# The mix stage of a hybrid decoder step: operands split part by part between the tiles of the product above

## The chip, the cores and the metric

The program runs on one core of a Trainium2 chip. The metric is the time of one execution on the device, in microseconds; for several runs the median is given. A profiled execution gives one trace: each instruction's start and length on TensorE (PE, with its weight loads as PEld), VectorE (DVE), ScalarE (ACT), GpSimd (POOL) and on SyncE (SP), which issues nearly all of the DMAs, and the clock that TensorE was granted.

## The reference

One decoder layer is computed for 512 prompt tokens and 8 sample tokens, together 520 columns. Two token mixers run on one normalised input, a gated DeltaNet (result `o_a`) and a sparse attention (result `o_b`). Their results are merged, and a feed-forward part follows:

```python
gate_a, gate_b = jnp.split(jax.nn.sigmoid(g_merge), 2, axis=-1)
mixed = (gate_a * (o_a @ P['w_oa']) + gate_b * (o_b @ P['w_ob'])) @ P['w_out']
x = x + gt1 * _rms(mixed, P['norm_g'][1])
h = _rms(x, P['norm_g'][2]) * (1.0 + sc2) + sh2
gate, up = jnp.split(h @ P['w_gu'], 2, axis=-1)
x = x + gt2 * _rms((jax.nn.silu(gate) * up) @ P['w_down'], P['norm_g'][3])
```

All is float32; `w_oa`, `w_ob` and `w_out` are 1024 x 1024. The change lies in the second of these lines.

## The kernel before

Activations stand with features on the 128 partitions and tokens along them, as 8 parts (KD = 8) of 128 features x 520 tokens. A float32 product is made of three faster ones: each operand is split into a high half (a copy in the short format, made by ACT) and a low half (what is left, a subtraction on DVE), and PE adds up high x high, high x low and low x high. One output tile (128 features x 520 tokens) is thus 8 parts x 3 products x 2 halves of 260 tokens = 48 matmuls.

The class `Chain` runs a list of such products, its jobs. The stage "mix" is one chain of three jobs: `oa` (w_oa), `ob` (w_ob) and `out` (w_out), each of 2 passes x 4 tiles = 8 tiles. The gates are applied by DVE (L2169 for `oa`; L2174 and L2176 for `ob`, the second adds up the merged tile in `mg_sg`), and `mg_sg` is the operand of `out`.

Each engine has its own queue, and semaphores order them:

- SP (`run_loads`, L221): first the four loads of the gates from memory (L2161, 1040 KB each), then the weights. A ring has two places, each with the 256 columns of two tiles (1024 KB); a place is loaded again once DVE has split its second tile (semaphore `low`). The first two loads are issued in the stage ahead (L1556).
- ACT (`run_high`, L281): the high half of a tile's weights (`ahead`, L287; of the first tile L301) and of the operand's parts (`split`, L293). `ahead` for tile n waits until product n-2 is done, since there are two weight places.
- DVE (`run_low`, L306): the low half of the weights (`low`, L310) and of the parts (L316), and the gating.
- PE (`run_products`, L236): ahead of a job it waits for all of the job's 8 low parts (semaphore `x_low`), ahead of a tile for its low weights (`low`) and for a free place in PSUM (`free`).

The order of the splits is that of `splits_before` (L257). On ACT and DVE alike the stage begins with the 8 parts of `oa`, then the first tile's weights, then the 8 parts of `ob`, and then the loop of `steps` (L265): for each tile m, the weights of tile m+1 and then the gating of tile m. Between the loops of `ob` and `out` stand the 8 parts of `out`: they need the merged tiles, and ACT waits for the last of them before it splits the first (`extra[1]` at 8). The first gating of `oa` waits for all four gate loads:

```python
if i == 0:
    for n in range(4):
        v.wait_ge(gates_in[n], 16 + START)
```

The chains of the feed-forward part (`gu`, `dw`) use the same class with one job each and an operand that is split elsewhere (`source` is None).

Of the kernel before, what the change touches and what calls it, by code (L numbers as in the profile page):

```python
# [6 lines left out]
F32 = mybir.dt.float32  # L7
I32 = mybir.dt.int32
F32R = mybir.dt.float32r
ALU = mybir.AluOpType  # L10
ACT = mybir.ActivationFunctionType
# [4 lines left out]
KD = D // P  # L16
# [54 lines left out]
START = 1  # L71
# [97 lines left out]
class Chain:  # L169
# [66 lines left out]
    def run_products(self, pe):  # L236
        for job in self.jobs:
            xh, xl = job.pair
            if job.x:
                pe.wait_ge(self.x_low, job.x + START)  # L240
            with pe.Fori(0, job.iters) as t:
                for i in range(4):
                    b, j = i // 2, i % 2
                    pe.wait_ge(self.low, job.unit + 4 * t + i + 1 + START)
                    if not (job.halves and b):
                        pe.wait_ge(self.free[j], (job.freed + (t if job.halves else 2 * t + b)) + START)
                    k0 = b * job.K if job.halves else 0
                    for k in range(job.K):
                        for w, x in ((self.wh, xh), (self.wh, xl), (self.wl, xh)):
                            for c in range(2):  # L250
                                last = pe.matmul(  # L251
                                    self.ps[:, j, c, 0:HALF], w[:, j, k, :], x[:, k0 + k, c * HALF:(c + 1) * HALF],
                                    start=(k0 + k == 0 and w is self.wh and x is xh),
                                    stop=(k == job.K - 1 and w is self.wl and not (job.halves and b == 0)))
                    last.then_inc(self.done, 1)

    def splits_before(self, job):  # L257


        i = self.jobs.index(job)  # L260
        own = job.source is not None and (i == 0 or job.source_steps)
        after = self.jobs[i + 1:i + 2]
        return [job] if own else [], [j for j in after if j.source is not None and not j.source_steps]

    def steps(self, eng, job, ahead, empty):  # L265

        last_job = job is self.jobs[-1]
        with eng.Fori(0, job.iters - 1 if last_job else job.iters) as t:
            for i in range(4):
                ahead(job, t, i + 1)  # L270
                if empty:
                    empty(eng, self, job, t, i)
        if last_job:
            t = job.iters - 1
            for i in range(4):
                if i < 3:
                    ahead(job, t, i + 1)
                if empty:
                    empty(eng, self, job, t, i)

    def run_high(self, act):  # L281
        def ahead(job, t, i):
            n, b, j = job.unit + 4 * t + i, i // 2 % 2, i % 2
            if j == 0:
                act.wait_ge(self.loaded[b], (job.unit // 4 + t + i // 4 + 1) * 16 * self.per + START)
            act.wait_ge(self.done, n - 1 + START)
            act.activation(self.wh[:, j, 0:job.K], self.ring[:, b, 0:job.K, j * P:(j + 1) * P], ACT.Copy).then_inc(self.high, 1)  # L287

        def split(job):
            if job.source_steps:  # L290
                act.wait_ge(self.extra[1], job.source_steps + START)
            for k in range(KD):
                act.activation(job.pair[0][:, k], job.source[:, k], ACT.Copy).then_inc(self.x_high, 1)  # L293

        for job in self.jobs:
            own, after = self.splits_before(job)
            for other in own:
                split(other)
            if job is self.jobs[0]:
                act.wait_ge(self.loaded[0], 16 * self.per + START)  # L300
                act.activation(self.wh[:, 0, 0:job.K], self.ring[:, 0, 0:job.K, 0:P], ACT.Copy).then_inc(self.high, 1)  # L301
            for other in after:
                split(other)
            self.steps(act, job, ahead, job.act)

    def run_low(self, v):  # L306
        def low(job, t, i):
            n, b, j = job.unit + 4 * t + i, i // 2 % 2, i % 2
            v.wait_ge(self.high, n + 1 + START)
            v.tensor_tensor(self.wl[:, j, 0:job.K], self.ring[:, b, 0:job.K, j * P:(j + 1) * P],  # L310
                            self.wh[:, j, 0:job.K].bitcast(F32), ALU.subtract).then_inc(self.low, 1)

        def split(job):
            for k in range(KD):
                v.wait_ge(self.x_high, job.x - KD + k + 1 + START)
                v.tensor_tensor(job.pair[1][:, k], job.source[:, k], job.pair[0][:, k].bitcast(F32), ALU.subtract)\  # L316
                    .then_inc(self.x_low, 1)

        for job in self.jobs:
            own, after = self.splits_before(job)  # L320
            for other in own:
                split(other)
            if job is self.jobs[0]:
                low(job, 0, 0)
            for other in after:
                split(other)
            self.steps(v, job, low, job.dve)


def square_sums(ph, st):  # L330
# [1105 lines left out]
def attention(nc, io, st):  # L1436
# [4 lines left out]
    ident = consts[:, K_ID:K_ID + P]  # L1441
    steps = [(g, kv, i) for g in range(G) for kv in range(KV) for i in range(NCH)]
    N = len(steps)
    HALF_N = N // 2
    with Phase(nc, "att") as ph:
# [1149 lines left out]
```

## Time and profile before

| what | value |
|---|---|
| time, median of 3 runs | 1923.19 us (1921.03 to 2191.4) |
| profiled execution, its own time | 1924.08 us |
| its span, first to last instruction | 1922.6 us |
| TensorE's granted clock, mean over the span | 0.915 of full speed |
| PE busy | 1680.5 us (87%) |
| DVE busy | 744.9 us (39%) |
| ACT busy | 549.8 us (29%) |

A busy share is a mean over stages with different limits; for one stage, the waits and the order in time within it decide. Times in the rows are counted from the span's start. The mix stage runs from about 1295 us to 1455 us.

### The profile page before, as it was taken

The numbers are of one execution on the slowest core, as the hardware profiler recorded it, in microseconds if no ns is written. First come the engines' busy times: TensorE is split into PE (matmuls) and PEld (weight loads), VectorE is DVE, ScalarE is ACT, GpSimd is POOL, SyncE is SP. The second block draws the span as 40 slices with busy tenths as digits, with TensorE's granted clock in tenths as the row PEclk, the third lists the DMA queues.
The fourth block names the chain that finished last, engine by engine and source line by source line (L and its number), as shares of the span: only waits on it lengthen the run. The fifth ranks groups of instructions, "written<-read, shape, count | busy, mean of one in ns | idle before, by whom it ended". The sixth has DMA issues, their size and how long they took to land. (4 is left out here: it accounts for less than half of the span.)

```text
span 1922.6 us, 30114 instructions
## 1 busy us (share of the span) xinstructions
PE 1680.5 (87%) x11733; PEld 1484.7 (77%) x11733; DVE 744.9 (39%) x1290; ACT 549.8 (29%) x890; POOL 162.6 (8%) x177
## 2 busy tenths in 40 slices
PE   4899889889889889977788899898985899997996
PEld 2598888888888879866574454458985899997996
DVE  1244554554553421323414434434435333332223
ACT  3243333333333320210003333323133434332222
POOL 0012322322312201100000000000000000000000
PEclk9799989989999986986879999999997899998997
DMA  6422212212112132437532343244212233332211
GB/s 188 114 71 73 70 33 79 63 33 85 57 33 98 45 86 80 140 121 226 155 110 88 110 153 121 94 136 167 98 44 89 66 89 99 96 87 90 90 60 45
DMA packets 228688, 181.72 MB, mean 95 GB/s; under 512 B 8566, under 2 KB 221039, under 8 KB 228425
## 3 DMA queue, kind: packets, MB, share of 16 engines
q1 hardware_dynamic: 203434, 161.82, 27.8%
q10 hardware_dynamic: 25184, 18.96, 3.2%
q8 instruction: 43, 0.70, 0.1%
q14 instruction: 27, 0.22, 0.0%
HBM read 166.31 MB, written 23.02 MB: 98 GB/s over the span
## 5 line engine op out<-in xcount | busy, mean ns | idle before, releaser
L704 PE MATMUL dn_pg<-proj_xh,dn_wh 128*128 128x260 f32 x832 | 184.0, 297 | 6.5 <-DVE dn_wl L1003 6.0
L704 PE MATMUL dn_pg<-proj_xh,dn_wl 128*128 128x260 f32 x832 | 182.5, 296 | 0.0
L704 PE MATMUL dn_pg<-proj_xl,dn_wh 128*128 128x260 f32 x832 | 179.1, 293 | 0.0
L251 PE MATMUL gu_ps<-fh_xh,gu_wh 128*128 128x260 f32 x704 | 142.4, 284 | 19.1 <-DVE gu_wl L310 19.1
L251 PE MATMUL gu_ps<-fh_xh,gu_wl 128*128 128x260 f32 x704 | 142.4, 284 | 0.0
L251 PE MATMUL gu_ps<-fh_xl,gu_wh 128*128 128x260 f32 x704 | 142.3, 284 | 0.0
L704 PEld LDWEIGHTS dn_pg<-proj_xh,dn_wh 128*128 128x128 f32 x832 | 134.3, 195 | 8.3 <-DVE dn_wl L1003 7.1
L704 PEld LDWEIGHTS dn_pg<-proj_xh,dn_wl 128*128 128x128 f32 x832 | 134.2, 195 | 0.0
L704 PEld LDWEIGHTS dn_pg<-proj_xl,dn_wh 128*128 128x128 f32 x832 | 134.2, 195 | 0.0
L251 PEld LDWEIGHTS gu_ps<-fh_xh,gu_wh 128*128 128x128 f32 x704 | 109.2, 190 | 19.5 <-issue 19.5
L251 PEld LDWEIGHTS gu_ps<-fh_xh,gu_wl 128*128 128x128 f32 x704 | 109.2, 190 | 0.0
L251 PEld LDWEIGHTS gu_ps<-fh_xl,gu_wh 128*128 128x128 f32 x704 | 108.9, 189 | 0.0
L251 PE MATMUL mix_ps<-mg_xh,mix_wh 128*128 128x260 f32 x384 | 79.2, 288 | 16.5 <-DVE mix_wl L310 8.8
L310 DVE TENSOR_TENSOR gu_wl<-all_ring,gu_wh 128x1024 fp32r<-128x1024 f32 x44 | 53.9, 1226 | 83.1 <-ACT gu_wh L287 80.4
L251 PE MATMUL dw_ps<-ff_gated_high,dw_wh 128*128 128x260 f32 x352 | 72.2, 287 | 12.6 <-DVE dw_wl L310 12.6
L1718 ACT ACTIVATE att_lg<-att_lg,att_nm 128x128 f32<-128x128 f32 (+3 forms) x64 | 35.4, 553 | 163.9 <-DVE att_nm L1793 163.9
L251 PE MATMUL mix_ps<-mg_xl,mix_wh 128*128 128x260 f32 x384 | 78.7, 287 | 0.0
L251 PE MATMUL mix_ps<-mg_xh,mix_wl 128*128 128x260 f32 x384 | 78.6, 287 | 0.0
L251 PEld LDWEIGHTS mix_ps<-mg_xh,mix_wh 128*128 128x128 f32 x384 | 60.8, 193 | 17.0 <-issue 17.0
L1808 DVE COPY att_PT<-att_pT 128x256 f32<-128x256 f32 (+3 forms) x32 | 26.4, 824 | 117.7 <-PE att_pT L1581 117.7
L251 PE MATMUL dw_ps<-ff_gated_high,dw_wl 128*128 128x260 f32 x352 | 71.7, 285 | 0.0
L251 PE MATMUL dw_ps<-ff_gated_low,dw_wh 128*128 128x260 f32 x352 | 71.6, 285 | 0.0
(472 smaller groups left out, 3381.3 us busy)
## 6 DMA issues: line engine op xcount, KB each, us to landing
all_ring<-in_w_gu SPq DMA_DIRECT2D x44, 512.0 KB, 5.0
all_ring<-in_w_in SPq DMA_DIRECT2D x32, 512.0 KB, 6.9
att_ada<-in_w_ada SPq DMA_DIRECT2D x16, 1024.0 KB, 5.3
fd_ring<-in_w_down SPq DMA_DIRECT2D x8, 1408.0 KB, 6.2
all_ring<-in_w_in SPq DMA_DIRECT2D x10, 1024.0 KB, 5.3
fr_ada<-in_w_ada SPq DMA_DIRECT2D x8, 1024.0 KB, 8.7
dn_xs<-in_w_in SPq DMA_DIRECT2D x16, 512.0 KB, 3.7
all_ring<-in_cmp_w ACTq DMA_DIRECT2D x16, 512.0 KB, 4.5
```

The source lines that it names most:

```text
L251: last = pe.matmul(self.ps[:, j, c, 0:HALF], w[:, j, k, :], x[:, k0 + k, c * HALF:(c + 1) * HALF], start=(k0 + k == 0 and w is self.wh and ...
L310: v.tensor_tensor(self.wl[:, j, 0:job.K], self.ring[:, b, 0:job.K, j * P:(j + 1) * P], self.wh[:, j, 0:job.K].bitcast(F32), ALU.subtract). ...
L704: last = pe.matmul(pg[:, j, c, 0:HALF], w[:, j, k, :], x[:, k, c * HALF:(c + 1) * HALF], start=(k == 0 and term == 0), stop=(k == KD - 1 a ...
L1718: last = a.activation(row, row, ACT.Exp, bias=nm[:, n % 2, br:br + 1], accum_out=sm[:, n % 2, br:br + 1])
L1808: v.tensor_copy(PT[:, :, 0:i + 1, i * P:(i + 1) * P], pT[:, :, 0:i + 1, :]).then_inc(pt_ready, 1)
```

## The change

Four things are changed in `Chain`, and only chains whose jobs split their operand are touched, which is the mix stage alone.

- The first tile's weights are split ahead of the parts of `oa`, on ACT and on DVE.
- The 8 parts of `ob` are split one at a time in the 8 tiles of `oa`: part m after the weights of tile m+1 and the gating of tile m. The loop of `steps` is written out for `oa` and `ob`.
- The parts of `out` are split the same way in the tiles of `ob`, one tile late: part m-1 in tile m, and the last after the loop. ACT waits for the one merged tile that a part needs (`extra[1]` at k+1).
- PE no longer waits for all 8 low parts ahead of a job; in the first tile of each pass it waits ahead of each part for that part.

```diff
--- before.py
+++ after.py
@@ -236,8 +236,6 @@
     def run_products(self, pe):
         for job in self.jobs:
             xh, xl = job.pair
-            if job.x:
-                pe.wait_ge(self.x_low, job.x + START)
             with pe.Fori(0, job.iters) as t:
                 for i in range(4):
                     b, j = i // 2, i % 2
@@ -246,6 +244,8 @@
                         pe.wait_ge(self.free[j], (job.freed + (t if job.halves else 2 * t + b)) + START)
                     k0 = b * job.K if job.halves else 0
                     for k in range(job.K):
+                        if job.source is not None and i == 0:
+                            pe.wait_ge(self.x_low, job.x - KD + k + 1 + START)
                         for w, x in ((self.wh, xh), (self.wh, xl), (self.wl, xh)):
                             for c in range(2):
                                 last = pe.matmul(
@@ -259,12 +259,21 @@
 
         i = self.jobs.index(job)
         own = job.source is not None and (i == 0 or job.source_steps)
-        after = self.jobs[i + 1:i + 2]
-        return [job] if own else [], [j for j in after if j.source is not None and not j.source_steps]
-
-    def steps(self, eng, job, ahead, empty):
+        return [job] if own else []
+
+    def steps(self, eng, job, ahead, empty, part):
 
         last_job = job is self.jobs[-1]
+        follower = self.jobs[self.jobs.index(job) + 1:][:1]
+        if follower and follower[0].source is not None:
+            late = 1 if follower[0].source_steps else 0
+            for m in range(4 * job.iters):
+                ahead(job, m // 4, m % 4 + 1)
+                if empty:
+                    empty(eng, self, job, m // 4, m % 4)
+                if m >= late:
+                    part(follower[0], m - late)
+            return
         with eng.Fori(0, job.iters - 1 if last_job else job.iters) as t:
             for i in range(4):
                 ahead(job, t, i + 1)
@@ -286,22 +295,23 @@
             act.wait_ge(self.done, n - 1 + START)
             act.activation(self.wh[:, j, 0:job.K], self.ring[:, b, 0:job.K, j * P:(j + 1) * P], ACT.Copy).then_inc(self.high, 1)
 
+        def part(job, k):
+            if job.source_steps:
+                act.wait_ge(self.extra[1], k + 1 + START)
+            act.activation(job.pair[0][:, k], job.source[:, k], ACT.Copy).then_inc(self.x_high, 1)
+
         def split(job):
-            if job.source_steps:
-                act.wait_ge(self.extra[1], job.source_steps + START)
-            for k in range(KD):
-                act.activation(job.pair[0][:, k], job.source[:, k], ACT.Copy).then_inc(self.x_high, 1)
+            for k in range(KD - 1 if job.source_steps else 0, KD):
+                part(job, k)
 
         for job in self.jobs:
-            own, after = self.splits_before(job)
-            for other in own:
-                split(other)
+            own = self.splits_before(job)
             if job is self.jobs[0]:
                 act.wait_ge(self.loaded[0], 16 * self.per + START)
                 act.activation(self.wh[:, 0, 0:job.K], self.ring[:, 0, 0:job.K, 0:P], ACT.Copy).then_inc(self.high, 1)
-            for other in after:
+            for other in own:
                 split(other)
-            self.steps(act, job, ahead, job.act)
+            self.steps(act, job, ahead, job.act, part)
 
     def run_low(self, v):
         def low(job, t, i):
@@ -310,21 +320,22 @@
             v.tensor_tensor(self.wl[:, j, 0:job.K], self.ring[:, b, 0:job.K, j * P:(j + 1) * P],
                             self.wh[:, j, 0:job.K].bitcast(F32), ALU.subtract).then_inc(self.low, 1)
 
+        def part(job, k):
+            v.wait_ge(self.x_high, job.x - KD + k + 1 + START)
+            v.tensor_tensor(job.pair[1][:, k], job.source[:, k], job.pair[0][:, k].bitcast(F32), ALU.subtract)\
+                .then_inc(self.x_low, 1)
+
         def split(job):
-            for k in range(KD):
-                v.wait_ge(self.x_high, job.x - KD + k + 1 + START)
-                v.tensor_tensor(job.pair[1][:, k], job.source[:, k], job.pair[0][:, k].bitcast(F32), ALU.subtract)\
-                    .then_inc(self.x_low, 1)
+            for k in range(KD - 1 if job.source_steps else 0, KD):
+                part(job, k)
 
         for job in self.jobs:
-            own, after = self.splits_before(job)
+            own = self.splits_before(job)
+            if job is self.jobs[0]:
+                low(job, 0, 0)
             for other in own:
                 split(other)
-            if job is self.jobs[0]:
-                low(job, 0, 0)
-            for other in after:
-                split(other)
-            self.steps(v, job, low, job.dve)
+            self.steps(v, job, low, job.dve, part)
 
 
 def square_sums(ph, st):
```

## Rows read from the trace of the kernel before

**Rows 1.** The page's costliest groups: busy us, mean ns, idle before and who ended it.

```profile
L251 PE MATMUL mix_ps<-mg_xh,mix_wh 128*128 128x260 f32 x384 | 79.2, 288 | 16.5 <-DVE mix_wl L310 8.8
```

**Rows 2.** Timeline at the stage's start: start us, length us, engine, line, count, [idle before <-releaser].

```profile
1295.72 4.32 ACT L293 ACTIVATE mg_xh<-mixers_oaT 128x520 fp32r<-128x520 f32 x8 [0.77 <-PEq L108]
1296.39 4.97 DVE L316 TENSOR_TENSOR mg_xl<-mixers_oaT,mg_xh 128x520 fp32r<-128x520 f32 x8
1299.95 1.04 ACT L301 ACTIVATE mix_wh<-all_ring 128x1024 fp32r<-128x1024 f32 x1
1300.18 2.19 SPq L2161 DMA_DIRECT2D mg_sg<-merge_gates  x4
...
1301.28 1.21 DVE L310 TENSOR_TENSOR mix_wl<-all_ring,mix_wh 128x1024 fp32r<-128x1024 f32 x1
...
1302.62 0.80 PE L251 MATMUL mix_ps<-mg_xh,mix_wh 128*128 128x260 f32 x2 [8.11 <-DVE mix_wl L310]
```

**Rows 3.** Timelines of SP, DVE and PE: first weight loads, first gating, third tile.

```profile
1276.71 11.02 SPq L1556 DMA_DIRECT2D all_ring<-in_w_oa  x2
...
1315.11 0.70 DVE L2169 TENSOR_TENSOR mg_sg<-mix_ps,mg_sg 128x520 f32 x1 [6.60 <-DMA mg_sg<-merge_gates]
1315.73 1.22 DVE L310 TENSOR_TENSOR mix_wl<-all_ring,mix_wh 128x1024 fp32r<-128x1024 f32 x1
...
1317.07 0.50 PE L251 MATMUL mix_ps<-mg_xh,mix_wh 128*128 128x260 f32 x2 [0.67 <-DVE mix_wl L310]
```

**Rows 4.** DMA views: L2161's landings; issues at 1276 to 1288; issues at 1308.4 to 1308.8.

```profile
DMA to landing us min/median/max: 5.1/9.8/13.1
...
all_ring<-in_w_oa SPq DMA_DIRECT2D x2, 1024.0 KB, 5.3
...
all_ring<-in_w_oa SPq DMA_DIRECT2D x1, 1024.0 KB, 9.1
```

**Rows 5.** Timeline between the last tile of `ob` and the first of `out`.

```profile
1398.22 0.70 DVE L2174 TENSOR_TENSOR all_hT<-mix_ps,mg_sg 128x520 f32<-128x520 f32 x1 [3.08 <-PE mix_ps L251]
1399.08 0.70 DVE L2176 TENSOR_TENSOR mg_sg<-mg_sg,all_hT 128x520 f32 x1 [0.15 <-DVE all_hT L2174]
1399.82 4.32 ACT L293 ACTIVATE mg_xh<-mg_sg 128x520 fp32r<-128x520 f32 x8 [6.41 <-DVE mg_sg L2176]
...
1405.78 0.80 PE L251 MATMUL mix_ps<-mg_xh,mix_wh 128*128 128x260 f32 x2 [7.71 <-DVE mg_xl L316]
1406.38 0.64 PE L251 MATMUL mix_ps<-mg_xl,mix_wh 128*128 128x260 f32 x2
1406.81 0.64 PE L251 MATMUL mix_ps<-mg_xh,mix_wl 128*128 128x260 f32 x2
```

**Rows 6.** Windows on PE: length us, busy us (matmuls), granted clock, DMA share, GB/s.

```profile
1296.50:1297.00 0.50, 0.00 (x0) 0.81 0.00 0
...
1307.00:1307.50 0.50, 0.50 (x6) 0.95 1.07 399
...
1402.50:1402.75 0.25, 0.00 (x0) 0.75 0.00 0
...
1409.25:1409.50 0.25, 0.25 (x3) 0.60 0.99 348
...
1095.00:1095.50 0.50, 0.00 (x0) 0.93 1.08 385
```

**Rows 7.** Timeline, PE, in the attention stage: a shorter idle stretch.

```profile
1098.33 0.90 PE L1581 MATMUL att_pT<-all_consts,att_lg 128*128 128x128 f32 x3 [4.51 <-ACT att_lg L1726]
```

**Rows 8.** Timelines of one steady tile of `oa`, across its boundary: ACT, PE, PEld.

```profile
1351.97 1.07 ACT L287 ACTIVATE mix_wh<-all_ring 128x1024 fp32r<-128x1024 f32 x1 [4.70 <-PE mix_ps L251]
...
1346.01 0.40 PE L251 MATMUL mix_ps<-mg_xh,mix_wh 128*128 128x260 f32 x2
1346.25 0.41 PE L251 MATMUL mix_ps<-mg_xl,mix_wh 128*128 128x260 f32 x2
...
1345.89 0.31 PEld L251 LDWEIGHTS mix_ps<-mg_xh,mix_wh 128*128 128x128 f32 x2
```

## The prediction

> **What bounds the kernel now.** I read the page's costliest groups first: the first group of the mix stage's matmuls had 16.5 us of idle PE ahead of it [rows 1]. The timelines split that into three stops: 8.11 us at the stage's start [rows 2], 0.67 us ahead of the third tile [rows 3], 7.71 us between `ob` and `out` [rows 5]. Everywhere else in the stage PE is the bound: a steady tile takes 5.77 us (ACT's 1.07 us of work and 4.70 us of waiting for PE), its 48 matmuls start 0.12 us apart (two in 0.24), across the boundary of a tile too [rows 8]. So the change can act on these stops and on the clock around them, and on nothing else; the other chains run the same instructions as before.
>
> The reader should look at who ends the third stop of DVE, not of PE: at 1315.11 DVE had waited 6.60 us for the gate loads [rows 3]. In the kernel before PE is nearly as late as the gates (0.67 us of idle), so they hardly show in PE's rows. They decide what an earlier start is worth.
>
> **The boundary to `out`.** Before: the last product of `ob` ends at 1398.07 (1405.78 less 7.71), gating and addition take until 1399.78, then come 8 parts on ACT and DVE, and PE starts at 1405.78 [rows 5]. After: parts 0 to 5 are split during the tiles of `ob`, and PE goes on at once. It wants part 6 after 36 matmuls (1398.07 + 36 x 0.12 = 1402.4) and part 7 after 42 (1403.1). DVE does the gating at 1398.22, the addition at 1399.08, then part 6 until about 1400.4 (a part takes 4.97 / 8 = 0.62 us of its queue [rows 2]); ACT has split part 7 by 1399.82 + 0.6 = 1400.4, DVE's half of it ends at 1401.3. Both are early, by 2.0 and 1.8 us. Next late would be the second tile's weights: ACT to 1401.5, then 0.29 us to DVE (1299.95 + 1.04 to 1301.28 [rows 2]) and 1.22 us, 1403.0, against PE's need at 1398.07 + 5.77 = 1403.8. If that cover of 0.8 us were gone, PE would wait for the rest of it alone. So the whole 7.71 us go.
>
> The clock adds to it. It fell at 1402.62 (0.75 in a window of a quarter of a us means half of it at half speed) and came back at 1409.45 [rows 6], 3.67 us after PE began again. At half clock two matmuls take 0.43 us (1406.38 to 1406.81 [rows 5]), at full clock 0.24 [rows 8]: 3.67 x (1 - 0.24 / 0.43) = 1.62 us. Sum at this boundary: 7.71 + 1.62 = 9.33 us saved.
>
> **The start.** ACT begins at 1295.72 [rows 2] now with the first weights, which it doesn't have to wait for: their load was issued at 1276.71 [rows 3], a load of this kind lands 5.3 us later [rows 4]. High half to 1296.76, low half from 1297.05 to 1298.26, DVE's first part to 1298.95, and with 0.13 us from DVE to PE (1301.28 + 1.21 to 1302.62 [rows 2]) PE starts at 1299.1, 3.5 us earlier than now. It follows the parts without a stop: at half clock (the clock fell at 1296.81 [rows 6]) a part is 6 x 0.215 = 1.3 us on PE, and ACT and DVE make one in 0.62. Two tiles, with about 4 us of them at half clock as now, end at about 1299.1 + 7.55 + 5.77 = 1312.4.
>
> The third tile can't start then. Its low weights stand on DVE behind the gating of tile 0, and that waits for the gates. The change doesn't touch SP's issue at 1300.18 [rows 2]. The first ring load behind the gates does come 4.0 us earlier (it waits for the second tile's low weights, now at about 1298.26 + 8 x 0.62 + 1.21 = 1304.4, before at 1308.5). In the rows, loads land in order of issue: the gates at about 1314.8 (the last of the four, issued some 0.6 us ahead of 1302.4, took 13.1 us), the ring load at 1308.5 + 9.1 = 1317.6 [rows 2, 4], so I take 0 for this; the bound is 2.8 us, if the two shared the time. DVE gates at 1315.11 as before, and now has part 0 of `ob` ahead of the weights: 1315.73 becomes 1316.35, and PE starts its third tile at 1317.69 instead of 1317.07 [rows 3]. That is 0.62 us lost where a naive sum has a gain.
>
> PE has then stood still for 5.3 us. The clock fell 2.3 us after the last matmul in the first stop (1294.51 to 1296.81 [rows 2, 6]), 4.55 us after it in the one at `out` [rows 5, 6] and 1.6 us after it in a stop of 4.51 us in the attention stage (1093.82 to 1095.43 [rows 6, 7]); all three are shorter than 5.3, so I let it fall. After the stage's two restarts it was low for 4.43 us (1302.62 to 1307.05) and 3.67 us [rows 2, 5, 6]; the mean, 4.05, costs 4.05 x 0.442 = 1.79 us. Its bounds are 0 (no fall) and 1.96. Before, this place ran at full clock. Sum at the start: 0.62 + 1.79 = 2.41 us lost.
>
> **What is added and hidden.** In the tiles of `oa` ACT does 1.07 + 0.62 us and DVE 1.22 + 0.70 + 0.62 of the tile's 5.77; in those of `ob` DVE does 1.22 + 0.86 + 0.70 + 0.62 = 3.4 us. Behind ACT's new wait for a merged tile stand the weights of the tile after next, which wait for a product 5.77 us later than the one that gates this tile; behind DVE's wait for a part stand those weights' low halves, with 2.3 us to spare. Writing the loop out adds no instruction that runs. PE's new waits are 8 in each of 6 tiles; the first of each 8 falls together with the two waits that every tile has, so 42 stand between matmuls. The price of a wait that is already met has no row of its own; the nearest is the boundary of a tile, where two such waits leave the 0.12 us between matmuls as it is [rows 8]. So I take 0. The upper bound is a weight load that no longer overlaps: two of them take 0.31 us at 0.12 apart, so one takes 0.19 [rows 8], 42 x 0.19 = 8.0 us. A gain from these waits is excluded, since PE's work is the same.
>
> The Trainium skill (TensorE: Matmul & The Clock Gate, Step-by-step: what each phase is for) says that PE pulls the next weight load ahead of matmuls in flight; it doesn't say whether a wait between them stops that. If it did, the sum would be the second rival's; by the boundary rows it would stay as it is.
>
> **Sum.** 9.33 - 2.41 = 6.92 us saved: 1924.08 - 6.92 = 1917.2 for the profiled execution. The median of the runs is 0.89 below that execution, so 1916.3.
>
> **The rivals.**
> - The gates don't bind, because they land earlier or because DVE gets to the weights: PE goes on at 1312.4 instead of 1317.07, the clock stays up, 9.33 + 4.67 = 14.0 us, 1909.2. For it: the page names DVE's weights as what PE waited for, 8.8 us [rows 1]. Against it: DVE's 6.60 us for the gates [rows 3], and that DVE's order has the gating first.
> - The waits break PE's flow: 42 x 0.19 = 8.0 us lost, 8.0 - 6.92 = 1.1 us slower, 1924.3. The place is the first tile of each pass; it ends slower from 6.92 / 42 = 0.165 us for a wait on. For it: PE loads weights ahead [rows 8]; against it: the tile boundaries.
> - The clock doesn't fall in the new stop: 9.33 - 0.62 = 8.71 us, 1914.5. For it: in the stop at `out` it held for 4.55 us [rows 5, 6], near to 5.3.
> - The earlier ring load delays the gates by the full 2.8 us: 4.1 us saved, 1919.1. Against it: the order of landing [rows 4].
> - The change doesn't do what it says at `out`, because a part or the second tile's weights come late: each us over the covers named above is a us less.
>
> **How the numbers follow.** The forecast 0.60, the clock held 0.14, the gates delayed 0.08, the gates not binding 0.06, the waits 0.06, late parts and the rest 0.06. The range reaches from below the held clock to past the delayed gates, with about 1.5 us for the spread of runs (1921.03 and 1923.19 lie 2.2 apart): 1912.3 to 1921.3. No case comes near 2% (38 us, about what a measurement of this kernel can tell from no change): faster 0.01, same 0.98, slower 0.01.
>
> **What would show it.** In the changed trace: PE's first matmul of the stage about 3.5 us earlier; an idle stop of about 5 us ahead of the third tile, with DVE's gating of tile 0 still begun about 0.3 us after the last gate, and half clock behind it; matmuls 0.12 us apart through the first tiles of `ob` and `out`, and no stop between `ob` and `out`. The prediction is wrong if the third tile starts straight after the second, if the spacing widens every 6 matmuls in the first tile of a pass, or if PE stops at part 6 or 7 of `out`.

## The result, and the profile after

The changed kernel takes 1909.0 us (median of 4 runs, 1907.29 to 1914.12), the kernel before, with one run more, 1923.74 us. One of the four runs of the kernel before, 2191.4 us, was a slow one; it counts in that median (1923.19 without it) and not in the ratio. The ratio is 0.9934, with a 95% interval of 0.9907 to 0.9961: 0.7% less time. The forecast was 1916.3 with a range from 1912.3 to 1921.3, so the time lies below the range. The profiled execution went from 1924.08 to 1914.12 us, by 10.0, and its span from 1922.6 to 1912.8.

The page has, in place of the 16.5 us of [rows 1]:

```profile
L251 PE MATMUL mix_ps<-mg_xh,mix_wh 128*128 128x260 f32 x384 | 79.1, 288 | 7.6 <-DVE mg_xl L325 4.3
```

Timelines of the changed kernel at the stage's start (against [rows 2, 3]), columns as there:

```profile
1296.37 1.06 ACT L311 ACTIVATE mix_wh<-all_ring 128x1024 fp32r<-128x1024 f32 x1 [0.77 <-PEq L108]
1297.34 4.31 ACT L301 ACTIVATE mg_xh<-mixers_oaT 128x520 fp32r<-128x520 f32 x8
...
1298.61 4.96 DVE L325 TENSOR_TENSOR mg_xl<-mixers_oaT,mg_xh 128x520 fp32r<-128x520 f32 x8
1303.49 1.21 DVE L320 TENSOR_TENSOR mix_wl<-all_ring,mix_wh 128x1024 fp32r<-128x1024 f32 x1
1314.33 0.70 DVE L2180 TENSOR_TENSOR mg_sg<-mix_ps,mg_sg 128x520 f32<-128x520 f32 x1 [9.63 <-DMA mg_sg<-merge_gates]
1314.95 0.69 DVE L325 TENSOR_TENSOR mg_xl<-all_obT,mg_xh 128x520 fp32r<-128x520 f32 x1
1315.56 1.22 DVE L320 TENSOR_TENSOR mix_wl<-all_ring,mix_wh 128x1024 fp32r<-128x1024 f32 x1
...
1299.44 0.77 PE L251 MATMUL mix_ps<-mg_xh,mix_wh 128*128 128x260 f32 x2 [4.27 <-DVE mg_xl L325]
...
1316.91 0.50 PE L251 MATMUL mix_ps<-mg_xh,mix_wh 128*128 128x260 f32 x2 [3.37 <-DVE mix_wl L320]
```

The first stop shrank from 8.11 to 4.27 us, and a stop of 3.37 us stands ahead of the third tile, where 0.67 us were. DVE's wait for the gates grew from 6.60 to 9.63 us, one part of `ob` (L325) stands between the gating and the third tile's weights, and PE begins when these are done. That is what was forecast, but the gating begins 19.16 us after the end of attention (1314.33 less 1295.17, which is 1299.44 - 4.27), and before it was 20.60 (1315.11 less 1294.51 [rows 2, 3]). The first two tiles took 14.10 us (1299.44 to 1313.54, which is 1316.91 less 3.37).

Between `ob` and `out` (against [rows 5]):

```profile
1399.24 0.40 PE L251 MATMUL mix_ps<-mg_xh,mix_wh 128*128 128x260 f32 x2
1399.48 0.41 PE L251 MATMUL mix_ps<-mg_xl,mix_wh 128*128 128x260 f32 x2
...
1399.44 0.70 DVE L2185 TENSOR_TENSOR all_hT<-mix_ps,mg_sg 128x520 f32<-128x520 f32 x1 [2.59 <-PE mix_ps L251]
1400.17 0.70 DVE L2187 TENSOR_TENSOR mg_sg<-mg_sg,all_hT 128x520 f32<-128x520 f32 x1
1400.79 1.49 DVE L325 TENSOR_TENSOR mg_xl<-mg_sg,mg_xh 128x520 fp32r<-128x520 f32 x2
1402.53 1.23 DVE L320 TENSOR_TENSOR mix_wl<-all_ring,mix_wh 128x1024 fp32r<-128x1024 f32 x1 [0.25 <-ACT mix_wh L296]
...
1400.91 0.64 ACT L301 ACTIVATE mg_xh<-mg_sg 128x520 fp32r<-128x520 f32 x1 [5.13 <-DVE mg_sg L2187]
1401.45 1.04 ACT L296 ACTIVATE mix_wh<-all_ring 128x1024 fp32r<-128x1024 f32 x1
```

The stop is gone: the product of `ob` ends at about 1399.3 and the matmuls stay 0.12 us apart. The last two parts are done at 1402.28, two us ahead of PE's need (1399.3 + 42 x 0.12 = 1404.3), the second tile's weights at 1403.76, 1.3 ahead of theirs. Windows on PE (as [rows 6]) show the clock:

```profile
1304.50:1305.00 0.50, 0.50 (x6) 0.85 0.99 387
1318.00:1318.50 0.50, 0.50 (x6) 0.80 0.00 0
1321.50:1322.00 0.50, 0.50 (x6) 0.79 1.02 360
1395.00:1411.00 16.00, 16.00 (x135) 1.00 0.23 77
```

After the first stop it came back at 1304.65 (0.15 us of that half us at half speed), 5.2 us after PE began. It fell again at 1318.3 (0.2 us of the half us at half speed), though PE had begun again at 1316.91, and rose at 1321.71: 3.4 us at half speed behind the new stop. Around `out` it now stays up.

### The profile page after: what moved, and what is told of

It is laid out like the page before. It is cut to its first block and busy times, and to the rows that moved or that the text cites. A ratio compares the mean times of both kernels' runs of the same rounds, so it can differ in the third digit from the quotient of the medians.

```text
span 1912.8 us, 30036 instructions
## 1 busy us (share of the span) xinstructions
PE 1674.1 (88%) x11733; PEld 1480.1 (77%) x11733; DVE 743.8 (39%) x1290; ACT 550.4 (29%) x890; POOL 162.4 (8%) x177
## 5 line engine op out<-in xcount | busy, mean ns | idle before, releaser
L1093 DVE TENSOR_TENSOR dn_M<-dn_M,dn_A 128x256 f32<-128x256 f32 x48 | 20.2, 421 | 124.5 <-PE dn_A L774 124.5
```

Source lines behind the costliest of these rows:

```text
L1093: v.tensor_tensor(even.rearrange("p (c n) s -> p c n s", c=NCH), even.rearrange("p (c n) s -> p c n s", c=NCH), y.rearrange("p c (n s) -> ...
```

## The experiments

All times of the stage below are read in the same way in each trace: from the last matmul of attention (the stage's first PE row less its idle time) to the first matmul of the stage, of its third tile, of `out`, and to the start of the last matmul of the stage. "Ahead" is the time from the span's start to the end of attention, "behind" the time from the stage's last matmul to the end. The ratio is to the kernel before, timed beside it.

| kernel | ahead | first | third tile | out | last | behind | ratio (95%) |
|---|---|---|---|---|---|---|---|
| before | 1294.5 | 8.11 | 22.56 | 111.27 | 159.02 | 469.0 | |
| before, again | 1304.6 | 8.12 | 22.64 | 111.35 | 159.04 | 468.7 | 0.9987 (0.9967 to 1.0007) |
| before, 96 waits | 1294.6 | 8.11 | 21.72 | 110.33 | 158.48 | 468.7 | one run, 1923.34 us |
| start alone | 1299.6 | 4.28 | 21.67 | 111.92 | 159.35 | 468.6 | 1.0003 (0.9979 to 1.0028) |
| end alone | 1303.7 | 8.11 | 22.52 | 103.36 | 149.37 | 467.5 | 0.9951 (0.9933 to 0.9970) |
| changed | 1295.2 | 4.27 | 21.73 | 104.07 | 150.08 | 467.5 | 0.9934 (0.9907 to 0.9961) |
| changed, again | 1285.6 | 4.28 | 21.68 | 104.03 | 150.04 | 468.1 | 0.9936 (0.9919 to 0.9954) |
| changed, third | 1293.0 | 4.28 | 21.62 | 103.97 | 149.98 | 467.2 | 0.9948 (0.9922 to 0.9975) |
| changed, waits in all tiles | 1289.8 | 4.27 | 21.87 | 104.19 | 150.20 | 467.0 | 0.9948 (0.9922 to 0.9973) |
| changed, gates one by one | 1288.6 | 4.28 | 18.01 | 98.74 | 144.75 | 469.3 | 0.9909 (0.9875 to 0.9943) |

Two theories stood at first. One: the stage gives about 9 us, the rest of the 14.7 us between the medians is drift elsewhere. Two: the edit moves something outside of the stage in every execution.

**The kernel before, again** (`b_again`, no edit).

> The kernel before, unchanged, timed against itself, to see what a difference of nothing looks like. Both theories expect a ratio of 1.000. Theory one (the stage accounts for about 9 us, the rest of the 14.7 us between the medians is drift of the half-clock stretches in stages that the edit doesn't touch) expects single executions to lie several us apart, and the parts of the trace ahead of the mix stage to differ by some us from the first trace of the same kernel, while the mix stage stays at 159.0 us from the end of attention to its last matmul. Theory two (the edit moves something outside the stage in every execution) expects the stages ahead of it to repeat within 1 us.

Measured: 1919.77 us, median of 12 executions (1915.78 to 1933.89), beside 24 others of the same kernel from 1911.01 to 1934.76. The stage repeats to 0.02 us, while the time ahead of it is 10.0 us longer. Windows on PE of the stages ahead, first of the first trace, then of this one (columns as [rows 6]):

```profile
170.00:300.00 130.00, 115.54 (x912) 0.95 0.16 45
300.00:435.00 135.00, 122.28 (x973) 0.95 0.22 62
```

```profile
170.00:300.00 130.00, 116.38 (x877) 0.91 0.16 45
300.00:435.00 135.00, 120.64 (x917) 0.91 0.22 62
```

Both traces are of one kernel, and these stretches were granted 0.95 of the clock in one execution and 0.91 in the other. So a few us between two executions, and between the medians of a few, say nothing about the edit; the stage's own time says it to 0.1 us.

**The changed kernel, again, twice** (`a_again`, `a_third`, no edit).

> The changed kernel, unchanged, timed again. Theory one expects the gain to come down from 14.7 us towards the stage's own 8.9 us (150.1 instead of 159.0 us from the end of attention to the last matmul of the stage), 9 to 12 us, ratio about 0.995. Theory two expects about 14 us again, ratio 0.9925, with the stages outside of mix shorter by 5 us in the trace.

> The changed kernel, unchanged, a third time, since the first ten executions lie 13 us under the kernel before on the mean and the stage gives 9.0. If the rest is chance (the half-clock stretches ahead of the stage fall otherwise in each execution), the mean goes towards 9 us. If the edit makes the rest shorter too, it stays at 13, and the stages ahead of mix are shorter than 1295 us in the trace again (1285.6 in the second trace, 1295.2 in the first).

Measured: 1910.01 (6 executions) and 1911.18 us (12), ratios 0.9936 and 0.9948. The stage takes 150.04 and 149.98 us. On its own the first repeat spoke for theory two: 13.5 us between the medians (1923.47 and 1910.01), and 1285.6 us ahead of the stage, 8.9 less than in the first trace of the kernel before. The second gave 11.0 us (1922.19 and 1911.18; 10.2 between the means), with 1293.0 us ahead. The three windows of the whole program, of before and of the changed kernel's first trace:

```profile
0.00:1294.50 1294.50, 1125.06 (x7293) 0.91 0.33 99
1294.50:1453.50 159.00, 142.51 (x1152) 0.95 0.28 93
1453.50:1922.50 469.00, 412.94 (x3291) 0.92 0.28 83
```

```profile
0.00:1295.20 1295.20, 1120.79 (x7293) 0.91 0.33 99
1295.20:1445.30 150.10, 142.49 (x1152) 0.97 0.30 99
1445.30:1912.70 467.40, 410.85 (x3290) 0.93 0.28 83
```

The mean of 22 executions of the changed kernel is 1911.35 (standard deviation 5.0), that of 59 of the kernel before 1922.83 (5.2): 11.5 us, with an uncertainty of 2.5 (twice the root of 5.0² / 22 + 5.2² / 59). The stage gives 9.0. Behind it, four traces of the kernel before's end (469.0, 468.7, 468.7, with the start alone 468.6) and four of the changed one's (467.5, 468.1, 467.2, 467.0) differ by 1.3 us on the mean. The rest, 1.2, is within the uncertainty. Ahead of the stage the five traces with the whole change have 1285.6 to 1295.2 us, the other five 1294.5 to 1304.6, which looks like theory two; but a trace is one execution out of the spread, and the three of the kernel before lie 0.5 to 11.1 us above its mean. So what is shown is the stage's 9.0 us. The 1.3 behind it are seen, but not their cause, and nothing ahead of it is told from chance.

**The end alone** (`out_only`).

```diff
-        if follower and follower[0].source is not None:
+        if follower and follower[0].source_steps:
             late = 1 if follower[0].source_steps else 0
...
+            if job.x and not job.source_steps:
+                pe.wait_ge(self.x_low, job.x + START)
...
-                        if job.source is not None and i == 0:
+                        if job.source_steps and i == 0:
```

The order of the splits in `oa`, and of the first weights, is that of the kernel before.

> Only the last part of the change: the parts of out are split in the tiles of ob, and PE waits for them one by one in the first tile of a pass; the stage's start and the parts of ob are as before. By my reading the stage keeps its stop of 8.1 us at the start and the third tile at 22.6 us, and loses the 7.7 us stop with 1.6 to 1.9 us of half clock: 9.4 us faster, so 0.5 to 0.7 us more than the whole change. If instead the two parts of the change each gave their naive share, this one would give 9.4 and the whole change 14.

Measured: the stage takes 149.37 us, 9.65 less than before and 0.7 less than the whole change; 1914.11 us, ratio 0.9951. The first stop and the third tile are as before. Of the 9.65, 7.91 are gone by the first matmul of `out` (111.27 less 103.36) and 1.74 in `out` itself, where the clock no longer falls.

**The start alone** (`start_only`).

```diff
-        if follower and follower[0].source is not None:
-            late = 1 if follower[0].source_steps else 0
+        if follower and follower[0].source is not None and not follower[0].source_steps:
+            late = 0
...
-                act.wait_ge(self.extra[1], k + 1 + START)
+                act.wait_ge(self.extra[1], job.source_steps + START)
...
-            for k in range(KD - 1 if job.source_steps else 0, KD):
+            for k in range(KD):
...
+            if job.source_steps:
+                pe.wait_ge(self.x_low, job.x + START)
...
-                        if job.source is not None and i == 0:
+                        if job.source is not None and i == 0 and not job.source_steps:
```

> Only the start: the first weights ahead of the parts of oa, the parts of ob in the tiles of oa, PE following the parts of oa and ob; the parts of out are split all together behind ob, and PE waits for all of them, as before. By my reading PE starts 3.8 us earlier, then stands 3 to 5 us ahead of the third tile until the gates have landed and DVE has done one more part, and runs 3.4 us at half clock: 0.5 to 2.4 us slower than before. If the gates didn't bind, it would be 4.5 us faster.

Measured: the stage takes 159.35 us, 0.33 more than before, though PE starts 3.8 us earlier; ratio 1.0003. The start alone buys nothing: 3.84 us come off the first stop, and the next one and the clock take them back. PE's row ahead of the third tile, and the clock after `out` has begun at 1411.55:

```profile
1321.30 0.50 PE L253 MATMUL mix_ps<-mg_xh,mix_wh 128*128 128x260 f32 x2 [3.49 <-DVE mix_wl L322]
```

```profile
1414.50:1415.00 0.50, 0.50 (x6) 0.95 1.09 356
```

The two parts nearly add up: -9.65 + 0.33 = -9.32, against -8.95 for both. Most of the difference lies in `out`, which still stops here: the clock came back 3.0 us after `out` began (at 1414.55), in the kernel before 3.67, and `out` is 0.3 us shorter for it (47.43 against 47.75).

**The gates one by one** (`gates_each`). This takes the suspected wait away by waiting for less: the data of tile m lie in gate load m // 4.

```diff
             if i == 0:
-                for n in range(4):
-                    v.wait_ge(gates_in[n], 16 + START)
+                v.wait_ge(gates_in[t], 16 + START)
...
             j, m = i % 2, 4 * t + i
+            if i == 0:
+                v.wait_ge(gates_in[2 + t], 16 + START)
```

> The changed kernel, with one difference: DVE waits ahead of tiles 0 to 3 of oa for the first gate load alone, ahead of tiles 4 to 7 for the second, and in ob for the third and the fourth in the same way. If the gates bind the third tile, as I hold, its stop of 3.4 us goes and so does the half clock behind it (3.4 us x 0.442 = 1.5): the stage takes 145.2 us from the end of attention to its last matmul instead of 150.1, 4.9 us less. If the stop has another cause (the weights, the free place in PSUM), nothing changes.

Measured: 144.75 us for the stage, 5.3 less than the changed kernel, 3.7 of it by the start of the third tile (21.68 less 18.01) and the rest behind it; 1904.79 us, ratio 0.9909, the fastest kernel of the study. The view of the tile `mix_ps` lists for whom its engine sat idle (us, times); of the gates and of DVE's weights nothing is left in it:

```profile
its engine sat idle before it (us, times) until:
  PE mix_ps L251: 77.9, 24
  issue: 4.4, 1
  DVE mg_xl L325: 4.3, 1
```

DVE's first gating now follows the product:

```profile
1301.11 0.70 DVE L2179 TENSOR_TENSOR mg_sg<-mix_ps,mg_sg 128x520 f32<-128x520 f32 x1 [2.96 <-PE mix_ps L251]
```

The gates bound the third tile. Its low weights and its place in PSUM both stand behind the gating of tile 0 and were late with it, not for a cause of their own.

**Waits in all tiles** (`waits_all`).

```diff
-                        if job.source is not None and i == 0:
+                        if job.source is not None:
```

> The changed kernel with PE's waits for the parts in all 24 tiles of the stage instead of 6: 144 waits more, all met long before. By my price of 0 the stage stays at 150.1 us. By the price of a weight load that no longer overlaps (0.19 us) it takes 27 us more.

Measured: 150.20 us, against 149.98 to 150.08. These 0.1 to 0.2 us are not the price of the waits. They lie in the stop ahead of the third tile, 3.60 us instead of 3.37 to 3.41, which DVE behind the gates ends:

```profile
1311.72 0.48 PE L251 MATMUL mix_ps<-mg_xh,mix_wh 128*128 128x260 f32 x2 [3.60 <-DVE mix_wl L320]
```

From there to the last matmul stand 136 of the 144 waits, and that takes 128.33 us (150.20 less 21.87), in the three traces of the changed kernel 128.35 to 128.36. So the waits cost nothing that shows. Fifteen us of steady tiles hold as many matmuls with them, first, as without:

```profile
1345.00:1360.00 15.00, 15.00 (x127) 1.00 0.21 71
```

```profile
1345.00:1360.00 15.00, 15.00 (x127) 1.00 0.44 138
```

**96 waits ahead of the stage** (`b_pad`). Why did the gates land earlier with the new start? SP issues them at the same time (1300.18 before, 1300.84 after, with attention ending 0.65 us later). The DMA view of the kernel before, from 1301.2 to 1314.2 (packets, MB, share of 16 engines by queue), shows one load of instructions among the gates:

```profile
q1 hardware_dynamic: 2620, 4.78, 101.9%
q8 instruction: 1, 0.02, 0.5%
```

In the changed kernel's, from 1301.9 to 1313.6, there is none:

```profile
q1 hardware_dynamic: 2180, 4.33, 100.7%
```

The edit puts 96 instructions into PE's queue, in a place where PE has nothing to do, so that PE's instruction loads come at other times:

```diff
     def run_products(self, pe):
+        if len(self.jobs) > 1:
+            for _ in range(96):
+                pe.wait_ge(self.done, START)
         for job in self.jobs:
```

> The kernel before, with 96 waits that are already met at the head of PE's part of the mix stage, where PE stands idle anyway. In the traces of the kernel before and of the one with the end alone, a 16 KB load of instructions starts 11.4 us after the end of attention, among the gate loads, and the last gate packet lands at 19.7 us; in the kernels with the new start that load comes at 1 to 5 us, and the last gate packet at 18.4. If that load holds up one of the 16 engines, moving it by 96 instructions brings the gates 1.3 us earlier here too, and DVE begins the first gating about 19.2 us after attention instead of 20.6. If the gates come earlier for another reason (SP, the ring load), they stay at 20.6. A second reading: 96 waits on PE in a row cost PE's start nothing.

Measured: the gating begins 19.22 us after attention (1313.84 less 1294.61) instead of 20.60, and the third tile starts 0.84 us earlier than before. The timeline of DVE:

```profile
1313.84 0.70 DVE L2172 TENSOR_TENSOR mg_sg<-mix_ps,mg_sg 128x520 f32 x1 [5.22 <-DMA mg_sg<-merge_gates]
```

The DMA view from 1301.3 to 1313.0 has the gates' queue alone:

```profile
q1 hardware_dynamic: 2197, 4.35, 102.4%
```

PE's first matmul is still 8.11 us behind attention. In all ten traces the last packet of the gates ends late (19.7 to 19.8 us after attention) where a 16 KB instruction load starts 11.3 to 11.5 us after it (three traces: before twice, and the end alone), and early (18.2 to 18.5) in the seven where none starts among them. In the late three the last 14 to 16 packets of the gates come one by one, 0.08 to 0.09 us apart, from 18.5 us on; in the other seven none is left by then. That one of the 16 DMA engines has fallen behind fits this, but it is my reading: the trace doesn't name the engine. Nor does it say whose instructions a load brings; that they are PE's is taken from the edit, which changes PE's queue alone.

## Why the prediction was wrong, step by step

- **What bounds.** Right: three stops of PE, and the gates behind the second. The sentence that the change can act on these and on nothing else was wrong by a little: behind the stage the granted clock came out otherwise. In the 70 us after the stage's last matmul it is 0.76 in both traces of the kernel before and 0.80 in the changed one's first. First before, then changed:

```profile
1453.50:1523.50 70.00, 41.78 (x279) 0.76 0.31 91
```

```profile
1445.20:1515.20 70.00, 41.48 (x283) 0.80 0.31 91
```

  The time behind follows this clock in all ten traces: 468.6 to 469.3 us at 0.76 (the kernel before twice, the start alone, the gates one by one), 468.1 and 468.7 at 0.78 (the changed kernel again, the 96 waits), 467.0 to 467.5 at 0.80 (the end alone, the changed kernel first and third, the waits in all tiles). The kernel with the gates one by one has the whole edit and the shortest stage and is at 0.76, so the edit doesn't by itself bring the gain, and its cause is not shown.
- **The boundary to `out`.** Right in mechanism and nearly in size: 9.33 us forecast, 9.65 measured with the end alone. The last part came two us early as forecast, the second tile's weights 1.3 us instead of 0.8.
- **The start.** Right in mechanism, including its sign: starting earlier gains nothing. The size was off: 2.41 us lost forecast, 0.33 measured alone, 0.7 in the whole change (-8.95 against -9.65). The term that was mis-sized is "DVE gates at 1315.11 as before": the gates land 1.4 us earlier, since the new instructions move PE's instruction load out of their way. The third tile so starts 0.83 us earlier than before instead of 0.62 later. The stop is 3.37 us instead of 5.3 for that, and since the first two tiles took 14.10 us instead of 13.3 (5.2 us of them at half clock, not about 4), against which PE's earlier start (3.84 us instead of 3.5) counts 0.3 the other way. The clock did fall (1.5 us lost for 3.4 at half speed, 1.79 forecast), only not in the stop: 1.4 us after PE had begun again. The rival of the delayed gates is out: the ring load went out at 1304.73 instead of 1308.54, and the gates came earlier, not later.
- **The waits.** Right: 0 was taken, nothing that shows was measured for 136 of them, and the rival that makes them 0.19 is out. The Trainium skill (TensorE: Matmul & The Clock Gate, Step-by-step: what each phase is for) has PE load weights ahead of matmuls in flight; by the spacing of 0.12 us, which stays, a wait that is met doesn't stop that.
- **The rival without binding gates** gave 1909.2, the measured number almost to the digit, and is wrong: the traces show the stop, and `gates_each` takes it away for 5.3 us more.
- **The sum and the range.** The stage saved 8.95 us instead of 6.92, 2.0 more, and 1.7 of them are the start's. With the stage sized rightly the forecast would have been 1914.2, inside the range. The step that failed is the one from the profiled execution to the median of the runs: "The median of the runs is 0.89 below that execution", with "about 1.5 us for the spread of runs (1921.03 and 1923.19 lie 2.2 apart)". The profiled execution took 1914.12 us, 3.1 less than the 1917.2 forecast: 2.0 in the stage, about 1.5 behind it, 0.7 lost ahead of it, and 0.2 outside the span (9.96 us off the execution's own time, 9.8 off its span). The median of its four runs was then 5.1 below it instead of 0.89, which is 4.2 of the 7.3 us by which the forecast missed. Single executions of one kernel have a standard deviation of 5 us and lie between 1911 and 1935, so that a median of three or four is known to about 3 us (an estimate from that deviation); the range allowed 1.5 for it. The gain, 14.7 us between the first medians, came down to 11.5 ± 2.5 between the means of 22 and 59 executions, of which the stage's 9.0 and the 1.3 behind it make 10.3. That the rest of the first 14.7 was drift ahead of the stage is likely by this and not shown run by run.

What stays open: why the clock behind the stage comes out at 0.76 in some traces and at 0.80 in others, and whether the us between 10.3 and 11.5 is more than chance.

## What to carry to other kernels

Taking work off the front of a stage moves the next thing that is late to the front; look for who waits behind it even if little of it shows now: here DVE's wait for the gates, of which PE's rows had 0.67 us. When a wait for several loads binds, wait for the one that the tile needs. The new start alone gave nothing, and that edit on top of it 5.3 us; without the new start it had only the stop of 0.67 us to take away (not run). And size an edit by its stage in the trace, which repeats to 0.1 us, not by a few whole runs, which differ by ten.

## What the runs showed that I hadn't expected

- Where a single 16 KB load of instructions fell among the gate loads, DVE's gating began 1.4 us later; 96 instructions that do nothing moved it away, and the third tile came 0.84 us earlier.
- A wait on PE that is already met costs nothing that shows between matmuls (128.33 us with 136 more of them, 128.35 to 128.36 without).
- Two executions of one kernel were granted 0.95 and 0.91 of TensorE's clock over the same 130 us, and differed by 10.0 us ahead of the mix stage.
- The clock can fall after PE has begun again: PE stood from 1313.54 to 1316.91 and the clock went to half at 1318.3.
